# One attention layer of a four-layer backbone: a head's value products placed between the score tiles of the next head

## The reference, cut to what matters

```
s = jnp.einsum('bhgqd,bhkd->bhgqk', qblk, k) * ATTN_SCALE
p = jax.nn.softmax(s, axis=-1).astype(v.dtype)
return jnp.einsum('bhgqk,bhkd->bhgqd', p, v)
```

## Time and profile before

| what | value |
|---|---|
| median of three runs | 2762.94 us (2761.91 to 2763.06) |
| the profiled execution's own time | 2762.46 us |
| its span | 2760.8 us |
| PE busy | 2678.9 us, 97% of the span |
| DVE busy | 1737.3 us, 63% |
| ACT busy | 851.0 us, 31% |
| chain that ended last, by engine | PE 90%, DVE 5%, ACT 2%, issue 2%, DMA 1% |
| granted PE clock, mean | 0.99 of 2.4 GHz |
| the 40 score tiles with their value products | from about 1400 to 1515.4 us of the span |

### The profile page before, as it was taken

One profiled execution on the slowest core, in us unless ns is written; L12 is line 12 of the kernel. 1 busy time (PEld: TensorE's weight loads), 2 busy tenths in 40 slices (PEclk: granted clock), 3 DMA queues, 4 the chain that ended last, 5 costly groups with the idle time before them and its releaser, 6 DMA issues.

```text
span 2760.8 us, 46246 instructions
## 1 busy us (share of the span) xinstructions
PE 2678.9 (97%) x17692; PEld 2615.9 (95%) x17692; DVE 1737.3 (63%) x2907; ACT 851.0 (31%) x1147; POOL 115.6 (4%) x206
## 2 busy tenths in 40 slices
PE   7999999999989999999988999999999999999997
PEld 7998999999979999999955999999999999999996
DVE  6888868675567776745664577768465554334345
ACT  3222332322343233124344432331242233223122
POOL 1000000000010000000000000000000000000000
PEclk9999999999999999999999999999999999999998
DMA  7344335343213443412100244434122222222211
GB/s 282 130 138 151 124 128 183 129 152 113 77 48 133 155 148 129 152 65 82 43 1 10 106 136 151 154 129 152 60 86 70 75 73 75 74 76 76 70 68 61
DMA packets 83867, 294.37 MB, mean 107 GB/s; under 512 B 9920, under 2 KB 11200, under 8 KB 83520
## 3 DMA queue, kind: packets, MB, share of 16 engines
q1 hardware_dynamic: 57424, 197.14, 21.3%
q0 software_dynamic: 26352, 95.96, 10.2%
HBM read 290.17 MB, written 2.88 MB: 106 GB/s over the span
## 4 chain that ended last, share of the span: by engine, by line
PE 90%; DVE 5%; ACT 2%; issue 2%; DMA 1%; DVEq 0%; ACTq 0%; POOL 0%; POOLq 0%
PE ps L414 42%; PE ps L415 42%; PE ps_x L612 1%; PE ps L591 1%; DVE w_lo L940 1%; DVE g_lo L954 1%; ACT w_hi L695 1%; DVE tmp L1011 1%; DVE tmp L1022 1%; DMA ada_w<-in_ada_w 1%; PE ps L467 1%; PE ps_sum L602 0%; DVE ps_x L968 0%; DVE h_lo L1078 0%; PE ps_x L579 0%
## 5 line engine op out<-in xcount | busy, mean ns | idle before, releaser
L940 DVE TENSOR_TENSOR w_lo<-raw,w_hi 128x1024 fp32r<-128x1024 f32 (+2 forms) x360 | 430.0, 1195 | 683.8 <-ACT w_hi L695 679.6
L695 ACT ACTIVATE w_hi<-raw 128x1024 fp32r<-128x1024 f32 (+2 forms) x360 | 372.5, 1036 | 939.8 <-PE ps L415 938.9
L414 PE MATMUL ps<-h_hi,w_hi 128*128 128x320 f32 x1888 | 592.0, 314 | 4.3 <-DVE h_lo L1078 2.9
L415 PE MATMUL ps<-h_lo,w_hi 128*128 128x322 f32 x1888 | 586.8, 311 | 0.0
L414 PE MATMUL ps<-h_hi,w_lo 128*128 128x320 f32 x1888 | 586.4, 311 | 0.0
L415 PE MATMUL ps<-h_hi,w_lo 128*128 128x322 f32 x1888 | 585.9, 310 | 0.0
L415 PE MATMUL ps<-h_hi,w_hi 128*128 128x322 f32 x1888 | 584.8, 310 | 0.0
L414 PE MATMUL ps<-h_lo,w_hi 128*128 128x320 f32 x1888 | 583.9, 309 | 0.0
L968 DVE CUSTOM_DVE_ANT_0 ps_x<-ada_w,cond 128x1024 f32<-128x1024 f32 x366 | 450.5, 1231 | 48.1 <-DVE tmp L1011 16.4
L414 PEld LDWEIGHTS ps<-h_hi,w_hi 128*128 128x128 f32 x1888 | 355.0, 188 | 7.3 <-issue 5.6
L415 PEld LDWEIGHTS ps<-h_hi,w_hi 128*128 128x128 f32 x1888 | 359.2, 190 | 2.2 <-issue 1.7
(11 more groups left out here) (135 smaller groups left out, 2928.4 us busy)
## 6 DMA issues: line engine op xcount, KB each, us to landing
raw<-in_weights SPq DMA_DIRECT2D x324, 512.0 KB, 3.2
ada_w<-in_ada_w POOLq DMA_DIRECT2D x183, 512.0 KB, 3.5
raw<-in_weights SPq DMA_DIRECT2D x32, 384.0 KB, 2.9
mix<-in_ada_head SPq DMA_DIRECT2D x9, 512.0 KB, 9.0
x<-in_x SPq DMA_DIRECT2D x4, 640.0 KB, 9.8
out_y<-mix SPq DMA_DIRECT2D x8, 320.0 KB, 2.3
mix<-in_spread SPq DMA_DIRECT2D x1, 1088.0 KB, 7.6
cond<-in_cond SPq DMA_DIRECT2D x1, 1024.0 KB, 4.7
```

Source lines behind the costliest of these rows:

```text
L414: pe.matmul(ps[:, 2 * slot, 0:TA], w[:, slot, ws], a(k)[:, 0:TA], start=begin, stop=end)
L415: mm = pe.matmul(ps[:, 2 * slot + 1, 0:width - TA], w[:, slot, ws], a(k)[:, TA:width], start=begin, stop=end)
L695: act.activation(w_hi[:, j % 2, 0:tiles * P], raw[:, j, 0:tiles * P], ACT.Copy).then_inc(w_hi_ready, 1)
L940: dve.tensor_tensor(w_lo[:, j % 2, 0:tiles * P], raw[:, j, 0:tiles * P], w_hi[:, j % 2, 0:tiles * P].bitcast(F32), ALU.subtract).then_inc( ...
```

## The change

The helper for the value products takes a list of chunks (0 to 4 are the five sample products, 5 is the prompt product). PE calls it at every tile with the chunks of a table: none at n % 5 = 0, chunk 0 at 1, chunk 1 at 2, chunk 2 at 3, and chunks 3, 4 and 5 at 4. They belong to the head before the one whose tiles are then turned. Chunk 0 waits for that head's four sample tiles and for `g_ready` of the head before it; chunk 5 waits for the head's prompt tile. The last head still has all six in a row at the end. ACT's `mixed_hi` moves behind tile 4 or 9, DVE's `mixed_lo` behind tile 5 or 0 of the following pair. No instruction is added or left out, and no product changes its operands or its order of addition.

```
+MIX_CHUNKS = [(), (0,), (1,), (2,), (3, 4, 5)]
...
-                def mix_values(kv, base, hh):
-
-                    pe.wait_ge(prob_kept, 10 * base + (5 * hh + 5))
-                    pe.wait_ge(g_ready, 2 * base + (LAYER_G[layer] + hh))
-                    of_sample, of_prompt = prob_of[hh]
-                    for k in range(5):
-                        val = v_tok[:, kv, k * P:(k + 1) * P] if k < 4 else cache_v[:, kv, :]
-                        pe.matmul(ps_rot, val, of_sample[:, k, :], start=(k == 0), stop=(k == 4))
-                    pe.matmul(ps_mixed, v_tok[:, kv, TS:T], of_prompt, start=True, stop=True).then_inc(mixed_done, 1)
+                def mix_values(head, chunks):
+
+                    kv = head * KVH // HEADS
+                    of_sample, of_prompt = prob_of[head % 2]
+                    for k in chunks:
+                        if k == 0:
+                            pe.wait_ge(prob_kept, 5 * head + 4)
+                            pe.wait_ge(g_ready, LAYER_G[layer] + head)
+                        if k < 5:
+                            val = v_tok[:, kv, k * P:(k + 1) * P] if k < 4 else cache_v[:, kv, :]
+                            pe.matmul(ps_rot, val, of_sample[:, k, :], start=(k == 0), stop=(k == 4))
+                        else:
+                            pe.wait_ge(prob_kept, 5 * head + 5)
+                            pe.matmul(ps_mixed, v_tok[:, kv, TS:T], of_prompt, start=True, stop=True).then_inc(mixed_done, 1)
...
-                        if n == 1 and pair:
-                            mix_values((pair - 1) * KVH // (HEADS // 2), pair - 1, 1)
-                        if n == 6:
-                            mix_values(pair * KVH // (HEADS // 2), pair, 0)
+                        if pair or n >= 5:
+                            mix_values(2 * pair + n // 5 - 1, MIX_CHUNKS[n % 5])
                         turn_probs(pair, n)
-                mix_values(KVH - 1, HEADS // 2 - 1, 1)
+                mix_values(HEADS - 1, range(6))
...
-                        if n == 1 and not first:
+                        if n == 4 and not first:
                             mixed_hi(i - 1, 1)
-                        if n == 6:
+                        if n == 9:
                             mixed_hi(i, 0)
...
-                        if n == 2 and not first:
+                        if n == 0 and not first:
+                            mixed_lo(i - 1, 0)
+                        if n == 5 and not first:
                             mixed_lo(i - 1, 1)
-                        if n == 7:
-                            mixed_lo(i, 0)
...
                 pair(HEADS // 2 - 1, last=True)
+                mixed_lo(HEADS // 2 - 1, 0)
                 mixed_lo(HEADS // 2 - 1, 1)
```

## The result

The changed kernel takes 2745.81 us (median of 5 runs, 2744.87 to 2751.09) against 2763.06 us before (5 runs, 2761.91 to 2763.31). The ratio is 0.9942, 95% interval 0.9931 to 0.9952: faster by 0.6%. The forecast was 2747.4 us, range 2743.5 to 2752.

A forecast was written before the change was run, and what follows sets the result against it. In the attention stage no engine is full; PE, DVE and ACT wait for each other in turn. Terms -12.3, -2.5 and -0.7 sum to -15.5 us, 2746.9 on the profiled execution; the median, 0.48 higher, gives 2747.4 us, range 2743.5 to 2752.

The forecast's parts named there:

- The sign "88 to 89 us": Expected time from head 0's first product to the output projection if right, instead of 104.1 us.
- third term: Head 7's block: 6.0 us instead of 6.71, -0.7, taking it that the clock falls again; bounds 0 and -2.2.
- The walk: Prices carried through the three engines' order: 14.19 us per head before, 12.14 after, from 11.40 of PE work plus waits.
- The two waits: PE waits for exponentials ahead of scores: 0.25 us at the head's tile 3, 0.48 at the next head's tile 1.
- the 0.76 us for the loops: Time over six heads that the hardware loops add to the walk, 85.90 - 6 x 14.19, kept for the new order.
- First term: Head 0's first product to head 6's: 73.6 us instead of 85.90, -12.3.
- Second term: Head 6's first product to head 7's: 9.0 us instead of 11.53, -2.5, including 2.27 us of idle PE.
- The rival with the clock up: Clock stays up at the end: last block takes 4.51 us, total 2745.9 us; chance 0.28.
- Stumbling at each chunk: Four places per head each cost one more hand-over of about 0.3 us: head 13.3 us, total 2755; chance 0.12.
- Late `mixed_lo`: The bare hand-over of 2.27 us stands in all six heads: +13.6, 2761 us, no measurable change; chance 0.03.
- Clock inside the stage: Clock falls within the attention stage; at half of the stage, 42 us, the time is 2768 us; chance 0.03.
- the named case: The forecast itself, 2747.4 us, with the clock falling at head 7's block; chance 0.50.

The follow-up runs named there:

- the table experiment: Changed kernel with chunk 0 at tile 1, chunks 1 and 2 at tile 2, 3 at tile 3, 4 and 5 at tile 4: 2744.98 us, ratio 0.9938.
- the one block: Changed kernel with the six products again one block at tile 1 of the next head, `mixed_hi` and `mixed_lo` kept later: 2759.02 us, ratio 0.9988.
- the later `mixed_hi`: Changed kernel with ScalarE's `mixed_hi` one place later, behind the exponential TensorE waits for at tile 1: 2752.11 us.
- the experiment with the second score buffer: Changed kernel with the last head's six products in the two banks of the second score buffer: 2747.35 us, ratio 0.994.
- the kernel with `mixed_lo` late: Changed kernel with `mixed_lo` two tiles later on VectorE, behind tiles 2 and 7 in place of 0 and 5: 2772.71 us, ratio 1.0039.
- the second series: The changed kernel run once more without edits: 2750.23 us, ratio 0.9951.

## Why the prediction was right, and which term was mis-sized

- **What bounds the kernel.** Right. The waiting of the three engines for each other held the stage; PE went from 12.12 to 13.66 us busy in 14, and the rest of the program only shifted (1245.51 us behind the stage, both times). The sign "88 to 89 us" for the stage was missed (87.01), by the third term below.
- **The walk.** Right in its mechanism; the sum is closer than the parts. Heads of 12.14 us outside the loops and about 12.4 inside were forecast; measured are 12.25 us for the first, outside them, 12.29 for the next, and on average 12.27. The two waits are where they were expected: from the transposes at 1426.35 to the scores at 1427.15 are 0.80 us, of which 0.56 is work, so 0.24 is waiting (forecast 0.25), and from 1433.93 to 1434.94 are 1.01 us, so 0.45 (forecast 0.48). What the walk left out is small: scores that start after a wait hold PE for 1.16 to 1.18 us (1427.15 to 1428.31) instead of 1.08, which is 0.18 us per head with two such waits. What it had too much is the 0.76 us for the loops, of which the new order shows nothing (12.25 to 12.29 us inside them). The two errors cancel, about 0.8 us each over six heads. The same walk then gave the heads of the table experiment (12.0, measured 11.91), of the one block (13.5, measured 13.60) and of the later `mixed_hi` (12.9 to 13.0, measured 12.95).
- **First term**, -12.3: measured -12.31, by the luck just named. **Second term**, -2.5 with a bare hand-over of 2.27 us: measured -2.62. The hand-over itself is 2.20 us; that the experiment with the second score buffer saved 2.27 in all is a coincidence. The trace shows the wait as 2.04 us and not 2.20, since the drain of the transpose ahead of it counts as busy.
- **Third term**, -0.7 for head 7's block: mis-sized. It measured -2.12, and this is nearly the whole difference between the -15.5 of the sum and the -17.05 of the stage. The step that failed is "the new idle time of 2.27 us is as long, so I take it that the clock falls again". It did not in four profiles with this gap and dealt-out products (the change twice, the other table, the later `mixed_hi`), nor with a gap of 3.02 us; the last block took 4.5 us in all five. It did fall behind a gap of 2.04 us in the one-block kernel (last block 7.53 us), where PE had been sparsely busy ahead of it, as in the kernel before. I had named density on both sides and given it too little weight, but it is not the whole cause. The clock also fell behind the same gap in the kernel with `mixed_lo` late (last block 6.20 us), where PE had been busy 3.98 of the 4 us from 1512 to 1516, and ahead of 52.17 with work on both sides of a gap of 2.89 us. So why it stayed up here is open. The rival with the clock up (2745.9 us, chance 0.28) is what the profiled execution did, at 2745.81.
- **The median.** Its nearness to the forecast (2745.81 against 2747.4 us) is in part luck. The same kernel gave 2750.23 in the second series, 12.7 us below the kernel before and not 17.3, with the same stage; the forecast had no term for this scatter.
- **The rivals.** Stumbling at each chunk: no, in heads 0 to 5 a chunk between scores and transposes holds PE 0.86 to 0.90 us, as in the block (0.86). Late `mixed_lo`: not here, it ended at 1435.08, 1.04 us ahead of chunk 0 at 1436.12 (0.9 forecast); the experiment that took this cover away lost the whole gain and more. Clock inside the stage: not here, but real once PE waits 2.8 us per head; and the price I gave for the late `mixed_lo` (2761 us, "no measurable change") left it out: 2772.71 was measured. The rule quoted from the Trainium skill, TensorE: Matmul & The Clock Gate, section "A second HAM failure mode: psum-queue depth-cycling", did not apply to this change: the granted clock was 1.00 in every slice of the dealt-out stage. In the experiment with `mixed_lo` late, with waits of 2.7 to 2.8 us, the trace shows the behaviour it describes: the clock fell and came back behind five of six of them.
- **The chances.** One result cannot say that 0.50 for the named case was too high, but the profiles speak for the clock rival. Sign, size and range held.

## What to carry to other kernels

Where several engines take turns and none is full, write down what each is held by per job, start to start, walk the order once for the order that exists and check it against the trace, and only then walk the new order: here this gave the heads of four new orders within 0.15 us (the change, the other table, the one block, the later `mixed_hi`). A block of work that waits for nobody belongs where an engine would otherwise wait, in pieces of the size of those waits; and the engine that fetches its result must be placed so that its hand-over is done before the next piece needs the buffer, since that wait cost the whole gain here, and the clock too. At the last round there is no other work to hide a hand-over behind, and a second buffer that has just become free is worth looking for.

## What the runs showed of the hardware

- Identical waits of 2.82 us of PE, in the same loop, were followed by the granted clock at 1.00 in one head and at 0.59 over 4 us in the next. A gap of 3.02 us between dense work left it at 1.00, and one of 2.89 us between dense work was followed by 0.57 over 4 us. In these traces, neither the length of an idle time nor dense work around it foretells the clock; I leave open what else does.
- A fall of the clock inside the stage cost 1.2 to 1.5 us per head in the experiment with `mixed_lo` late, and 3.0 us in the last block of the one-block kernel (7.53 in place of 4.51 us).
- The same instructions, ahead of the stage, took 4.1 us longer in one execution than in another, all of it in the first 57 us, where PE worked at about half the pace until 43.5 us and not 35. For changes of 2 us in one stage, the stage's length in the trace repeated to 0.01 us (87.01 and 87.02; 82.64 and 82.65) where medians of five executions of one kernel moved by 4.4 us (2745.81 and 2750.23).
